# The expert loop's gelu is written back to PSUM, and the gating multiplies from there

## The chip, the core and the metric

The kernel runs on one core of a Trainium2 chip. The metric is the device time of one execution in microseconds (us). Three runs of the kernel before the change took 3090.99, 3093.1 and 3093.38 us; their median is 3093.1 us.

## The reference

One layer of a hybrid decoder for a prompt of 512 tokens (plus 16 learned ones) and 8 sampled tokens: RWKV-7 time mixing and differential attention side by side, gated, projected, and then a channel mixer with 16,384 experts of one neuron each. The change lies in that mixer alone:

```
q = (x @ peer_wq) ...; s = q . subkeys; top-16 of each half; top-16 of the 256 sums -> idx, gate
hid = einsum('td,thkd->thk', xb, u_tab[ib])
hid = gelu(hid, exact) * gate
out = einsum('thk,thkd->td', hid, v_tab[ib])
```

Each token uses 128 experts (8 heads of 16).

## The kernel before, in words

Everything is float32. TensorE products are made of float32r halves: a matrix is copied to a rounded "high" half, the difference is the "low" half, and three products (high by high, high by low, low by high) are summed in PSUM.

The expert mixer (`peer_experts`) treats 392 of the 520 token columns densely. For these, all 16,384 experts are computed, in 64 pairs of blocks of 128 experts. The gate matrix M of a pair, mostly zeros, comes from scratch memory. The remaining 128 tokens are treated row by row: in the first half of the loop (32 pairs) four rows of `peer_u` per pair are fetched by indirect DMA and multiplied with x (`few_dot`, L2038), and in the second half four rows of `peer_v` are fetched and added with their weights (`few_add`, L2054).

For one pair of the dense part, with e = 0, 1 the block in the pair, the steps are:

- TensorE transposes U in four steps into the PSUM tiles pU (`turn`, L1862). ScalarE copies each to the high half UH (`cut_u`, L1916), VectorE forms the low half UL (`rest_u`, L2023).
- TensorE computes the hidden values into the PSUM tile pH[e] (`product_u`, L1872, 24 matmuls for each e).
- ScalarE writes gelu of pH[e] to the SBUF tile G[e] (`gelu`, L1928). VectorE multiplies G[e] by M in place (`gate`, L2029). ScalarE copies G[e] to GH (`cut_g`, L1934), and GpSimd forms GL = G - GH (`rest_g`, L1971).
- ScalarE copies V to VH (`cut_v`, L1922), and GpSimd forms VL = V - VH, one instruction of 128x2048 (`rest_v`, L1975).
- TensorE multiplies VH, VL with GH, GL, eight output blocks of six matmuls each (`product_v`, L1883), and VectorE adds each block to the result (`add`, L2033).

The loop is pipelined over the pairs p, q = p+1 and r = p+2. Each engine has its own instruction queue, in an order written out by hand, and semaphores tie them together. In one step of the loop:

- TensorE: `product_u(q)`; then for n = 0 to 7 `product_v(p, n)`, with `turn(r, n/2)` ahead of each even n.
- ScalarE: `gelu(q,0)`, `cut_v(q)`, `cut_g(q,0)`, `gelu(q,1)`, `cut_u(r,0)`, `cut_g(q,1)`, `cut_u(r,1..3)`.
- VectorE: `gate(q,0)`, `gate(q,1)`; in the second half of the loop a small copy of 128x4 (`few_weigh`, L2047); then for even n `rest_u(r, n/2)` and `add(p,n)`, for odd n one `few_dot` or `few_add` and `add(p,n)`.
- GpSimd: `rest_v(q)`, `rest_g(q,0)`, `rest_g(q,1)`; then it waits until VectorE has used the four rows that share the buffer (the last `few_dot` or `few_add` of pair q), copies four row numbers (L1981), and issues four indirect DMAs (L1987) for pair q+2.
- SyncE issues the loads of U, M and V.

`product_v(p, n)` uses one of four PSUM tiles and so waits until `add(p, n-4)` is done; `turn(r, st)` with st of 2 or 3 waits for `rest_u(r, st-2)`.

Of the kernel before, what the change touches and what calls it, by code (L numbers as in the profile page):

```python
# [17 lines left out]
ALU = mybir.AluOpType  # L18
ACT = mybir.ActivationFunctionType
# [88 lines left out]
def sc(nc):  # L108
    return nc.scalar.activation
# [1325 lines left out]
ND = TQ - SPARSE  # L1435
# [323 lines left out]
def peer_experts(nc, ins, c, xh, xl, mscr, acc, few, spare):  # L1759
# [7 lines left out]
    with Stage(nc, "experts") as s:  # L1767
        U = [s.sb(f"U{b}", [P, 2, D]) for b in range(2)]
        V = [s.sb(f"V{b}", [P, 2, D]) for b in range(2)]
        M = [s.sb(f"M{b}", [P, 2, ND]) for b in range(2)]  # L1770
# [4 lines left out]
        G = [s.sb(f"G{e}", [P, ND]) for e in range(2)]  # L1775
# [9 lines left out]
        pH = [s.ps(f"pH{e}", [P, 512]) for e in range(2)]  # L1785
# [5 lines left out]
        turned, u_hi, u_lo, hidden, gelued, gated, g_hi, g_lo, v_hi, v_lo, summed, added = (  # L1791
            s.sem(n) for n in ("turned", "u_hi", "u_lo", "hidden", "gelued", "gated", "g_hi", "g_lo", "v_hi", "v_lo",
                               "summed", "added"))
# [71 lines left out]
        def product_u(pe, q):  # L1865
            for e in range(2):
                pe.wait_ge(u_lo, q.count(4, 2 * e + 2))
                if q.after(1):
                    pe.wait_ge(gelued, q.count(2, e - 1))
                for k in range(KD):  # L1870
                    for n, (u, x) in enumerate(((UH, xh), (UH, xl), (UL, xh))):
                        last = nc.tensor.matmul(pH[e][:, 0:ND], u[e][:, k, :], x[:, k, :], start=(k == 0 and n == 0),  # L1872
                                                stop=(k == KD - 1 and n == 2))
                last.then_inc(hidden, 1)
# [11 lines left out]
        @blk.tensor  # L1886
        def _(pe):
            def first():
                for st in range(4):
                    turn(pe, Pair(0), st)  # L1890
                product_u(pe, Pair(0))
                for st in range(4):
                    turn(pe, Pair(1), st)

            def body(p, q, r, rows_of_u):
                product_u(pe, q)
                for n in range(8):
                    if n % 2 == 0:
                        turn(pe, r, n // 2)
                    product_v(pe, p, n)  # L1900

            def tail():
                product_u(pe, Pair(NQ - 1))
                for p in (NQ - 2, NQ - 1):
                    for n in range(8):
                        product_v(pe, Pair(p), n)

            schedule(pe, first, body, tail)
# [14 lines left out]

        def gelu(act, q, e):
            act.wait_ge(hidden, q.count(2, e + 1))
            if q.after(1):
                act.wait_ge(g_lo, q.count(2, e - 1))
            sc(nc)(G[e][:, :], pH[e][:, 0:ND], ACT.Gelu).then_inc(gelued, 1)  # L1928

        def cut_g(act, q, e):  # L1930
            act.wait_ge(gated, q.count(2, e + 1))
# [5 lines left out]
        def _(act):  # L1937
            def hidden_values(q):
                gelu(act, q, 0)
                cut_v(act, q)  # L1940
                cut_g(act, q, 0)
                gelu(act, q, 1)
# [83 lines left out]
        def gate(dve, q, e):  # L2026
            dve.wait_ge(m_in[q.b], q.loads())
            dve.wait_ge(gelued, q.count(2, e + 1))
            nc.vector.tensor_tensor(G[e][:, :], G[e][:, :], M[q.b][:, e, :], ALU.mult).then_inc(gated, 1)  # L2029

        def add(dve, q, n):
            dve.wait_ge(summed, q.count(8, n + 1))
# [25 lines left out]
        def _(dve):  # L2058
            def first():
                dve.sem_inc(added, 4)  # L2060
                for st in range(4):
                    rest_u(dve, Pair(0), st)
                for e in range(2):
                    gate(dve, Pair(0), e)
                for st in range(4):
                    rest_u(dve, Pair(1), st)
                for n in range(NB):
                    few_dot(dve, Pair(0), n)
                few_keep(dve, Pair(0))

            def body(p, q, r, rows_of_u):
                for e in range(2):
                    gate(dve, q, e)
                if q.i is None and q.off == NQ // 2:
                    dve.wait_ge(few_gelued, 1)
                    nc.vector.tensor_tensor(hid[:, :], hid[:, :], few["gate"][:, :], ALU.mult).then_inc(few_gated, 1)
                    dve.wait_ge(few_gated, 1)
                if not rows_of_u:
                    few_weigh(dve, q)
                for n in range(8):  # L2080
                    if n % 2 == 0:
                        rest_u(dve, r, n // 2)
                    elif rows_of_u:
                        few_dot(dve, q, n // 2)
                    else:
                        few_add(dve, q, n // 2)
                    add(dve, p, n)
                if rows_of_u:
                    few_keep(dve, q)

            def tail():
                for e in range(2):
                    gate(dve, Pair(NQ - 1), e)
                few_weigh(dve, Pair(NQ - 1))
                for p in (NQ - 2, NQ - 1):
                    for n in range(8):
                        add(dve, Pair(p), n)
                        if p == NQ - 2 and n % 2:
                            few_add(dve, Pair(NQ - 1), n // 2)
# [178 lines left out]
```

## Time and profile before

| | us |
|---|---|
| median of 3 runs | 3093.1 |
| the profiled execution's own time | 3090.84 |
| its span in the trace | 3089.7 |
| PE busy | 2410.4 (78%) |
| DVE busy | 2033.2 (66%) |
| ACT busy | 775.1 (25%) |
| POOL busy | 1095.0 (35%) |

In the profile PE is TensorE (PEld its weight loads), DVE VectorE, ACT ScalarE, POOL GpSimd and SP SyncE. "Busy" is the time in which an engine executes an instruction, and an instruction's duration counts from its dispatch: time in which it is held up inside the engine counts as busy too. The expert loop takes the stretch from about 1640 us to 3076 us of the span, so it is nearly half of the kernel. The stretches before it are not touched by the change.

### The profile page before, as it was taken

To read this page: it belongs to the slowest core of one execution; us is meant where nothing else is said; L and a number is where in the kernel's file an instruction comes from. 1 tells how busy PE (TensorE), PEld (TensorE's weight loads), DVE (VectorE), ACT (ScalarE), POOL (GpSimd) and SP (SyncE) were. 2 spreads that over 40 slices of the span, in tenths; PEclk is the share of its full clock that TensorE was granted. 3 is DMA by queue.
4 is the path that set the end of the run, shared out by engine and by line. 5 is a ranking of instruction groups with operands and counts; after the bars stand their busy time and mean duration, and the time that the engine had idled before them with its cause. 6 is when DMAs were issued, how large, how long until landed. Compare 5 with 4: busy or idle time off the path is not lost. (4 is left out here: it accounts for less than half of the span.)

```text
span 3089.7 us, 49756 instructions
## 1 busy us (share of the span) xinstructions
PE 2410.4 (78%) x17079; PEld 2159.8 (70%) x17079; DVE 2033.2 (66%) x3749; ACT 775.1 (25%) x1389; POOL 1095.0 (35%) x1131
## 2 busy tenths in 40 slices
PE   4965885586969679604847999899988889889898
PEld 3964774244349678503637889888888888888887
DVE  3137554756731417998956776777778787787877
ACT  1111000122212211004953222222222222222221
POOL 2410000001313311326944545445454544545443
PEclk8976887665979889856978999999999999999999
DMA  2310000123812212100587556556555555555552
GB/s 65 88 36 1 3 3 21 41 83 101 271 46 72 70 55 62 34 0 0 138 194 285 205 201 214 204 201 211 199 199 211 206 198 200 201 207 205 199 199 94
DMA packets 207541, 403.48 MB, mean 131 GB/s; under 512 B 12798, under 2 KB 134073, under 8 KB 190810
## 3 DMA queue, kind: packets, MB, share of 16 engines
q1 hardware_dynamic: 165210, 251.21, 25.0%
q0 software_dynamic: 42240, 151.03, 14.6%
q8 instruction: 60, 0.98, 0.1%
q14 instruction: 31, 0.25, 0.0%
HBM read 370.81 MB, written 31.39 MB: 130 GB/s over the span
## 5 line engine op out<-in xcount | busy, mean ns | idle before, releaser
L2029 DVE TENSOR_TENSOR experts_G<-experts_G,experts_M 128x392 f32<-128x392 f32 x128 | 369.5, 2887 | 330.3 <-ACT experts_G L1928 330.2
L1883 PE MATMUL experts_pV<-experts_GH,experts_VH 128*128 128x392 f32 x1024 | 404.7, 395 | 27.9 <-DVE keep_xT L2033 27.2
L1883 PE MATMUL experts_pV<-experts_GL,experts_VH 128*128 128x392 f32 x1024 | 369.8, 361 | 0.0
L1883 PE MATMUL experts_pV<-experts_GH,experts_VL 128*128 128x392 f32 x1024 | 369.0, 360 | 0.0
L1872 PE MATMUL experts_pH<-keep_xh,experts_UH 128*128 128x392 f32 x1024 | 351.3, 343 | 0.0
L1872 PE MATMUL experts_pH<-keep_xl,experts_UH 128*128 128x392 f32 x1024 | 349.3, 341 | 0.0
L1872 PE MATMUL experts_pH<-keep_xh,experts_UL 128*128 128x392 f32 x1024 | 348.4, 340 | 0.0
L1975 POOL TENSOR_TENSOR experts_VL<-experts_V,experts_VH 128x2048 fp32r<-128x2048 f32 x64 | 295.3, 4614 | 19.3 <-ACT experts_VH L1922 18.0
L2033 DVE TENSOR_TENSOR keep_xT<-experts_pV,keep_xT 128x392 f32<-128x392 f32 x512 | 282.3, 552 | 1.6 <-PE experts_pV L1883 1.5
L1862 PE MATMUL experts_pU<-keep_ident,experts_U 128*128 128x128 f32 x1024 | 167.6, 290 | 117.2 <-DVE experts_UL L2023 109.0
L1883 PEld LDWEIGHTS experts_pV<-experts_GH,experts_VH 128*128 128x128 f32 x1024 | 208.2, 203 | 56.8 <-DVE keep_xT L2033 54.1
L1862 PEld LDWEIGHTS experts_pU<-keep_ident,experts_U 128*128 128x128 f32 x1024 | 132.2, 149 | 143.6 <-DVE experts_UL L2023 126.6
L1981 POOL COPY experts_at<-keep_few_row 128x4 uint32 (+1 forms) x64 | 11.8, 184 | 620.2 <-DVE experts_dot L2038 296.7
L1916 ACT ACTIVATE experts_UH<-experts_pU 128x512 fp32r<-128x512 f32 x256 | 151.7, 593 | 262.0 <-PE experts_pU L1862 262.0
L1883 PEld LDWEIGHTS experts_pV<-experts_GL,experts_VH 128*128 128x128 f32 x1024 | 210.6, 206 | 0.0
L1883 PEld LDWEIGHTS experts_pV<-experts_GH,experts_VL 128*128 128x128 f32 x1024 | 209.2, 204 | 0.0
L1872 PEld LDWEIGHTS experts_pH<-keep_xh,experts_UL 128*128 128x128 f32 x1024 | 192.9, 188 | 0.0
L1872 PEld LDWEIGHTS experts_pH<-keep_xh,experts_UH 128*128 128x128 f32 x1024 | 192.9, 188 | 0.0
L1872 PEld LDWEIGHTS experts_pH<-keep_xl,experts_UH 128*128 128x128 f32 x1024 | 192.8, 188 | 0.0
L1928 ACT ACTIVATE experts_G<-experts_pH 128x392 f32<-128x392 f32 x128 | 63.7, 497 | 481.7 <-PE experts_pH L1872 481.7
L2023 DVE TENSOR_TENSOR experts_UL<-experts_pU,experts_UH 128x512 fp32r<-128x512 f32 x256 | 173.1, 676 | 10.5 <-ACT experts_UH L1916 10.5
L1025 POOL IOTA att_dist<- 128x528 f32 x1 | 0.6, 572 | 460.2 <-POOLq L68 460.2
(424 smaller groups left out, 5164.3 us busy)
## 6 DMA issues: line engine op xcount, KB each, us to landing
experts_U<-in_peer_u SPq DMA_DIRECT2D x64, 1024.0 KB, 4.8
experts_V<-in_peer_v SPq DMA_DIRECT2D x64, 1024.0 KB, 5.2
experts_M<-scratch_gates SPq DMA_DIRECT2D x64, 392.0 KB, 3.2
keep_K<-in_cache_k SPq DMA_DIRECT2D x64, 256.0 KB, 3.1
keep_V<-in_cache_v POOLq DMA_DIRECT2D x64, 256.0 KB, 3.7
scratch_gates<-spread_M SPq DMA_DIRECT2D x2, 8192.0 KB, 33.0
inp_w<-in_w_in SPq DMA_DIRECT2D x22, 512.0 KB, 3.8
scratch_gates<-spread_M SPq DMA_DIRECT2D x1, 8704.0 KB, 35.6
```

What stands on the lines that cost most here:

```text
L1025: nc.gpsimd.iota(dist[:, :], pattern=[[-1, WM]], base=META + 3 * P, channel_multiplier=1, allow_small_or_imprecise_dtypes=True).then_inc(b ...
L1862: last = nc.tensor.transpose(pU[a][:, k, :], U[q.b][:, e, (4 * a + k) * P:(4 * a + k + 1) * P], c["ident"][:, :])
L1872: last = nc.tensor.matmul(pH[e][:, 0:ND], u[e][:, k, :], x[:, k, :], start=(k == 0 and n == 0), stop=(k == KD - 1 and n == 2))
L1883: last = nc.tensor.matmul(pV[n % 4][:, 0:ND], l, r, start=(t == 0), stop=(t == 5))
L1916: sc(nc)(UH[e][:, 4 * a:4 * a + 4, :], pU[a][:, :, :], ACT.Copy).then_inc(u_hi, 1)
L1928: sc(nc)(G[e][:, :], pH[e][:, 0:ND], ACT.Gelu).then_inc(gelued, 1)
L1975: nc.gpsimd.tensor_tensor(VL[q.b][:, :, :], V[q.b][:, :, :], VH[q.b][:, :, :].bitcast(F32), ALU.subtract).then_inc(v_lo, 1)
L1981: nc.gpsimd.tensor_copy(at[q.b][:, :], few["row"][:, bass.ds(q.count(NB, 0 if of_u else -SLOTS), NB)]).then_inc(staged, 1)
L2023: nc.vector.tensor_tensor(UL[e][:, 4 * a:4 * a + 4, :], pU[a][:, :, :], UH[e][:, 4 * a:4 * a + 4, :].bitcast(F32), ALU.subtract).then_inc( ...
L2029: nc.vector.tensor_tensor(G[e][:, :], G[e][:, :], M[q.b][:, e, :], ALU.mult).then_inc(gated, 1)
L2033: nc.vector.tensor_tensor(acc[:, n, :], pV[n % 4][:, 0:ND], acc[:, n, :], ALU.add).then_inc(added, 1)
```

## The change

The gelu no longer writes G[e] but overwrites its own input pH[e] in PSUM. The gating multiply reads pH[e] (PSUM) and M (SBUF) and writes G[e]. The waits follow the buffers: `product_u` of the next pair, which overwrites pH[e], waits for the gating (`gated`) where it waited for the gelu (`gelued`), and the wait for `rest_g` of the pair before (`g_lo`), which protects G[e], goes from the gelu on ScalarE to the gating on VectorE.

```diff
             for e in range(2):
                 pe.wait_ge(u_lo, q.count(4, 2 * e + 2))
                 if q.after(1):
-                    pe.wait_ge(gelued, q.count(2, e - 1))
+                    pe.wait_ge(gated, q.count(2, e - 1))
...
         def gelu(act, q, e):
             act.wait_ge(hidden, q.count(2, e + 1))
-            if q.after(1):
-                act.wait_ge(g_lo, q.count(2, e - 1))
-            sc(nc)(G[e][:, :], pH[e][:, 0:ND], ACT.Gelu).then_inc(gelued, 1)
+            sc(nc)(pH[e][:, 0:ND], pH[e][:, 0:ND], ACT.Gelu).then_inc(gelued, 1)
...
         def gate(dve, q, e):
             dve.wait_ge(m_in[q.b], q.loads())
             dve.wait_ge(gelued, q.count(2, e + 1))
-            nc.vector.tensor_tensor(G[e][:, :], G[e][:, :], M[q.b][:, e, :], ALU.mult).then_inc(gated, 1)
+            if q.after(1):
+                dve.wait_ge(g_lo, q.count(2, e - 1))
+            nc.vector.tensor_tensor(G[e][:, :], pH[e][:, 0:ND], M[q.b][:, e, :], ALU.mult).then_inc(gated, 1)
```

VectorE's queue at the head of a step of the loop, as a difference between before (-) and after (+). REGISTER_ALU and ISA rows are the queue's own preparation of waits:

```order
 L1825 UNCONDITIONAL_BRANCH
 L1825 ISA
-L2028 ISA
-L2029 TENSOR_TENSOR experts_G<-experts_G,experts_M 128x392
+L2026 ISA
 L2028 REGISTER_ALU
-L2029 TENSOR_TENSOR experts_G<-experts_G,experts_M 128x392
-L2022 ISA
-L2023 TENSOR_TENSOR experts_UL<-experts_pU,experts_UH 128x512
+L2029 TENSOR_TENSOR experts_G<-experts_pH,experts_M 128x392
+L2026 REGISTER_ALU
```

The compute instructions stand in the same order on every engine; only the gating's first operand and the place of one wait are new.

## Rows read from the trace of the kernel before

**Rows 1.** The page's costliest groups: busy us, mean ns of one, idle before
```profile
L2029 DVE TENSOR_TENSOR experts_G<-experts_G,experts_M 128x392 f32<-128x392 f32 x128 | 369.5, 2887 | 330.3 <-ACT experts_G L1928 330.2
...
L2033 DVE TENSOR_TENSOR keep_xT<-experts_pV,keep_xT 128x392 f32<-128x392 f32 x512 | 282.3, 552 | 1.6 <-PE experts_pV L1883 1.5
```
**Rows 2.** Timeline, all engines, pair at 1994 us: start, duration, instruction, idle before
```profile
1991.89 0.52 ACT L1934 ACTIVATE experts_GH<-experts_G 128x392 fp32r<-128x392 f32 x1
...
1994.53 6.07 DVE L2029 TENSOR_TENSOR experts_G<-experts_G,experts_M 128x392 f32<-128x392 f32 x1 [3.73 <-ACT experts_G L1928]
1994.59 4.61 POOL L1975 TENSOR_TENSOR experts_VL<-experts_V,experts_VH 128x2048 fp32r<-128x2048 f32 x1
...
1999.15 1.01 POOL L1971 TENSOR_TENSOR experts_GL<-experts_G,experts_GH 128x392 fp32r<-128x392 f32 x1
...
2001.24 1.04 POOL L1971 TENSOR_TENSOR experts_GL<-experts_G,experts_GH 128x392 fp32r<-128x392 f32 x1 [1.07 <-ACT experts_GH L1934]
...
2001.59 1.76 DVE L2038 CUSTOM_DVE_ANT_0 keep_xn<-keep_xn,keep_few_x 128x1024 f32<-128x1024 f32 x1
...
2010.21 1.21 DVE L2038 CUSTOM_DVE_ANT_0 keep_xn<-keep_xn,keep_few_x 128x1024 f32<-128x1024 f32 x1
...
2011.61 0.18 POOL L1981 COPY experts_at<-keep_few_row 128x4 uint32 x1 [9.33 <-DVE experts_dot L2038]
...
2017.12 4.63 POOL L1975 TENSOR_TENSOR experts_VL<-experts_V,experts_VH 128x2048 fp32r<-128x2048 f32 x1
```
**Rows 3.** Stretches of each half, L1975 alone: from:to, length, busy (count), clock
```profile
1683.40:2354.50 671.10, 138.42 (x30) 0.94 0.59 205
2354.50:3035.80 681.30, 138.54 (x30) 0.95 0.58 201
```
**Rows 4.** Timeline, TensorE: the first transposes of three successive steps, and one inner wait
```profile
2197.81 0.60 PE L1862 MATMUL experts_pU<-keep_ident,experts_U 128*128 128x128 f32 x4
...
2217.20 0.60 PE L1862 MATMUL experts_pU<-keep_ident,experts_U 128*128 128x128 f32 x4
...
2224.65 0.66 PE L1862 MATMUL experts_pU<-keep_ident,experts_U 128*128 128x128 f32 x4 [2.14 <-DVE experts_UL L2023]
...
2242.19 0.60 PE L1862 MATMUL experts_pU<-keep_ident,experts_U 128*128 128x128 f32 x4
```
**Rows 5.** Timeline, the loop's second pair, where a row product stands behind the port
```profile
1661.21 0.53 ACT L1934 ACTIVATE experts_GH<-experts_G 128x392 fp32r<-128x392 f32 x1
...
1662.06 4.60 POOL L1975 TENSOR_TENSOR experts_VL<-experts_V,experts_VH 128x2048 fp32r<-128x2048 f32 x1
1662.18 7.50 DVE L2038 CUSTOM_DVE_ANT_0 experts_R<-experts_R,keep_few_x 128x1024 f32<-128x1024 f32 x1
...
1666.61 1.97 POOL L1971 TENSOR_TENSOR experts_GL<-experts_G,experts_GH 128x392 fp32r<-128x392 f32 x2
```
**Rows 6.** Timeline, a pair in which the gating comes late
```profile
2196.00 0.52 ACT L1934 ACTIVATE experts_GH<-experts_G 128x392 fp32r<-128x392 f32 x1
2196.18 4.61 POOL L1975 TENSOR_TENSOR experts_VL<-experts_V,experts_VH 128x2048 fp32r<-128x2048 f32 x1
...
2198.62 2.60 DVE L2029 TENSOR_TENSOR experts_G<-experts_G,experts_M 128x392 f32<-128x392 f32 x1 [3.72 <-ACT experts_G L1928]
```
**Rows 7.** Timeline, the last pair: the small copy of 128x4
```profile
3060.58 2.35 POOL L1971 TENSOR_TENSOR experts_GL<-experts_G,experts_GH 128x392 fp32r<-128x392 f32 x2
3060.98 1.00 DVE L2047 COPY experts_dot<-experts_hid 128x4 f32<-128x4 f32 x1
```
**Rows 8.** Timeline, a pair of the second half
```profile
2604.01 4.63 POOL L1975 TENSOR_TENSOR experts_VL<-experts_V,experts_VH 128x2048 fp32r<-128x2048 f32 x1
...
2609.96 0.16 DVE L2047 COPY experts_dot<-experts_hid 128x4 f32 x1
...
2611.10 1.68 DVE L2054 SCALAR_TENSOR_TENSOR keep_few_y<-experts_R,experts_dot,keep_few_y 128x1024 f32<-128x1024 f32 x1
...
2626.82 4.62 POOL L1975 TENSOR_TENSOR experts_VL<-experts_V,experts_VH 128x2048 fp32r<-128x2048 f32 x1
```

## The prediction

> **What bounds the kernel now.** I read the costliest groups first, then the timeline of single steps of the expert loop on all engines, and last TensorE's own rows.
>
> The costliest VectorE group is the gating, L2029: 128 instructions with a mean of 2887 ns, beside L2033, which has the same shape, one operand in PSUM, and a mean of 552 ns over 512 instructions [rows 1]. A mean so far from that of a like instruction asks for the single ones. The step at 1994 us shows one: the gating of the second block is dispatched at 1994.53 and ends at 2000.60, 6.07 us later [rows 2]. GpSimd's split of V runs from 1994.59 to 1999.20, its first `rest_g` from 1999.15 to 2000.16, and the gating ends 0.44 us after that. So it does not compute for 6 us; it is held until GpSimd stops, and then takes its own half microsecond. Both read two operands from SBUF. The row product (`few_dot`) shows the same: dispatched at 2001.59 under GpSimd's second `rest_g` (to 2002.28), it takes 1.76 us against 1.21 us when GpSimd is quiet [rows 2]. L2033, which reads PSUM and one SBUF operand, shows nothing of the kind in its mean [rows 1].
>
> What sets the period of the loop is a ring through both engines. GpSimd starts the split of V at v = 1994.59. VectorE is held, and finishes its first row product at 2003.35, which is v + 8.76. Three further rounds bring the last row product to 2011.42, 8.07 us later (2.69 us a round). GpSimd, idle for 9.33 us until then, copies row numbers at 2011.61, issues four indirect DMAs, and starts the next split at 2017.12 [rows 2]: 5.70 us after the last row product. 8.76 + 8.07 + 5.70 = 22.53 us, the distance from v to v. The stretches give means of 671.10/30 = 22.37 us for the first half and 681.30/30 = 22.71 us for the second [rows 3]. The first is a bit below 22.53 because some steps have a late gating, as in [rows 6].
>
> TensorE is not the one that sets it: from 2197.81 to 2217.20 a step took 19.39 us, and the next 24.99 us, with a wait of 2.14 us for `rest_u` in it [rows 4]. The long step also ran in part at a lower clock: the granted clock of the stretches is 0.94 and 0.95 of the full 2.4 GHz [rows 3].
>
> **The change, part by part.**
>
> *The gelu* writes PSUM instead of SBUF. No row before shows ScalarE writing PSUM. The reads and writes of like size all lie near half a microsecond (the 128x392 copy at 1991.89 took 0.52 us [rows 2]), and I take no difference, with 0.2 us either way as bounds. It isn't in the ring: what follows it on VectorE is held by GpSimd for about 4 us more, so a later or earlier gelu moves nothing. Cost 0.
>
> *The waits.* TensorE's wait for the gating of the pair before is satisfied well before: TensorE writes pH again only behind the eight output blocks and four transposes of the step, and the gating is done by the middle of these (2201.22 against 2197.81, with the step's 19.39 us [rows 4, 6]). VectorE's new wait for `rest_g` of the pair before is for an instruction that ended at v + 7.69 (2002.28 [rows 2]), while the next step's gatings stand behind the eight adds and four row products, which end at 2011.42 or later. Behind the gating in VectorE's queue stand `rest_u`, the adds and the row products, so it would be dear if late, but it has that slack. Cost 0.
>
> *The gating itself* has now one SBUF operand, as L2033 has, so I price it at 0.55 us [rows 1] and free of the hold. For the block e = 0 nothing changes. For e = 1, 5.5 us leave VectorE's busy time in a fully held step.
>
> *What is late next.* The gating was only the first instruction to meet GpSimd's splits. The next instruction on VectorE with two SBUF operands now stands there.
>
> First half of the loop: after the gating come `rest_u` and `add`, 0.99 us from the gating's end to the row product's dispatch (2000.60 to 2001.59 [rows 2]), and neither is held. The row product is then dispatched about 0.55 + 0.99 = 1.5 us after the gating is, while the split of V still runs. That this instruction is held too is seen at 1662.18: 7.50 us, until both `rest_g` are through at 1668.58, and 1.10 us more [rows 5]. How many of GpSimd's three instructions it must let pass decides the gain. In [rows 2] the gating let two pass (both ready before v; the copy GH for the first was done at 1992.41). In [rows 5] all three were ready before v (GH of the second block was done at 1661.74), and all three passed. In [rows 6] the first `rest_g` became ready at 2196.52, 0.34 us after v, and the gating passed ahead of it, ending at 2201.22, 0.43 after the split. So I read: those of GpSimd's instructions go ahead that were ready when the split began. After the change GH of the second block is ready about 0.55 + 0.5 us after the gating's dispatch, and the gating comes 0.8 us after TensorE's first transpose of the step (2198.62 against 2197.81 [rows 4, 6]), that is near v as now. So the second `rest_g` is ready about 1 us after v, and two instructions pass. The row product ends at 5.57 (2000.16 - 1994.59) + 1.10 = v + 6.67. That is 8.76 - 6.67 = 2.09 us less than now, so the period is 20.44 us. Against the mean: (22.37 - 20.44) x 30 = 58 us.
>
> Second half: here the small copy L2047 stands between gating and `rest_u`. It reads one SBUF operand, but it is held as well: in the last pair it took 1.00 us under a `rest_g` [rows 7], against 0.16 us in [rows 8]. Now it comes after the long hold; after the change it comes first and takes the hold over. It ends near v + 5.6, and `few_add` is dispatched 1.14 us behind it (2609.96 to 2611.10 [rows 8]), at v + 6.71. The second `rest_g` runs meanwhile and is through by then. `few_add` takes 1.27 us when not held (the 1.68 in the row is held by the `rest_g` there; 1.21 is the like product of [rows 2], and I take 1.27 as 1.21 plus 5%, an estimate), so it ends at v + 7.98 against v + 8.77 now (2611.10 + 1.68 - 2604.01). The gain is 0.79 x 30 = 24 us.
>
> The Trainium skill, page "SBUF — State Buffer", section "Who interferes with whom", says that GpSimd shares a port pair with VectorE, that a VectorE instruction with two SBUF inputs, or a copy in a two-port mode, is blocked whole by a GpSimd one that reads SBUF, and that one with a single SBUF input outside these modes is not. The rows agree, the 1.00 us copy included. It also says that whoever issues first gets the pair. By that rule the second `rest_g`, ready before the row product is dispatched, would pass too; that is the first rival below.
>
> *The sum.* 58 + 24 = 82 us off the profiled execution's own 3090.84 us gives 3009 us. The median of the three runs is 2.3 us above that execution, so 3011 us. TensorE's 19.39 us lies below both new periods (20.4 and 21.9 us), so it does not cap the gain; at the loop's two ends TensorE is the bound or the steps are few, and I count nothing.
>
> **The rivals.**
>
> *All three of GpSimd's instructions pass.* For: [rows 5] has it. Against: they were all ready there before v, which [rows 6] suggests matters. The first row product would end at v + 7.62 (1669.68 - 1662.06): the period is 22.53 - 1.14 = 21.39, a gain of 0.98 x 30 = 29 us. In the second half the copy would end at v + 6.5 and `few_add` at 6.52 + 1.14 + 1.27 = v + 8.93, 0.16 us later than now, a loss of 5 us. Together 24 us: 3069 us.
>
> *More gets free.* In [rows 6] the gating, dispatched 2.44 us after v, passed after the split alone. If the row product does too, it ends at 4.6 + 1.1 = v + 5.7, then meets the second `rest_g` with its next product at about v + 7.7, and that one ends near v + 8.8 in place of 9.4; the period is 19.9 us, the gain of the first half 74 us, the second at 24 to 56 us: 2963 to 2995, say 2978 us. Were the copy not held at all, the second half would gain 2.0 x 30 = 60 us beside 58: 2975 us, the same neighbourhood.
>
> *TensorE becomes the bound* at 19.39 us a step, because GpSimd's four DMAs or the row products come early enough: (22.54 - 19.39) x 60 = 189 us, 2904 us. Against: the ring has 13.77 us beside the held piece, and nothing of it is touched.
>
> *The gating stays held* although it reads PSUM: then nothing changes, 3093 us. L2033's mean speaks against it.
>
> *Slower: TensorE's clock.* Waits inside each step may cost the clock. The step of 24.99 us had more than 2.14 us of waiting and then ran partly at half clock; against 19.39 it lost 24.99 - 19.39 - 2.14 = 3.46 us beyond that wait. Now such a step is followed by a short one, and the mean stays at 22.5. If the new hold, which falls once in every step on the row product and so on the adds that TensorE waits for, brought every step to 24.99 us, the loop would lose (24.99 - 22.54) x 60 = 147 us: 3240 us. It decides from the point at which TensorE's own step, with waits and low clock, is longer than the ring. Against: TensorE's wait shrinks by as much as its work stretches, since GpSimd's start depends on VectorE's and not on TensorE's pace.
>
> **How the numbers follow.** The forecast has 0.50, all three pass 0.21, more free 0.16, TensorE the bound 0.03, nothing changes 0.04, slower 0.04; 0.02 is left for cases unnamed. The forecast's own spread is about 15 us either way (1 us of error in one half's period is 30 us). The range 2965 to 3070 us takes in the forecast, the first rival's value, and most of the third case's. A change under 0.2%, or 6 us, could not be told from none. Faster 0.92, same 0.03, slower 0.05.
>
> **What would show it.** The gating's mean falls from 2887 to about 555 ns. The first row product of each step in the first half grows to about 5 us. In the second half the copy L2047 grows from 0.16 to about 5 us. GpSimd's idle before L1981 falls by the gain, and the splits of V follow each other at 20.4 and 21.9 us. If L2047 stays at 0.16, the second half is mispriced; if the row product ends at v + 7.6, the first rival holds; if TensorE's clock falls below 0.94 with longer steps, the last one.

## The result: 3059.0 us, two fifths of the gain that was forecast

The changed kernel takes 3059.0 us (median of 4 runs, 3058.19 to 3060.7), the kernel before, run beside it, 3092.05 us. The ratio is 0.9895, with a 95% interval of 0.9878 to 0.9912. It is faster by 33 us, where 82 us were forecast. The time lies in the range, near its slow end.

The groups that answer to [rows 1], from the page of the changed kernel; the third is the small copy of the loop's second half:

```profile
L2029 DVE TENSOR_TENSOR experts_G<-experts_pH,experts_M 128x392 f32<-128x392 f32 x128 | 72.5, 567 | 326.4 <-ACT experts_pH L1926 322.2
L2033 DVE TENSOR_TENSOR keep_xT<-experts_pV,keep_xT 128x392 f32<-128x392 f32 x512 | 282.6, 553 | 1.6 <-PE experts_pV L1883 1.5
...
L2047 DVE COPY experts_dot<-experts_hid 128x4 f32 (+1 forms) x32 | 171.0, 5344 | 0.0
```

The gating fell from a mean of 2887 ns to 567 ns, as forecast: 297 us of busy time are gone from that line. VectorE's busy time as a whole only fell from 2033.2 to 2006.6 us. The hold moved on. In the second half the copy of 128x4 carries it, 5344 ns a piece.

The timeline of a step in the first half, all engines (answers to [rows 2]):

```profile
2000.93 4.63 POOL L1973 TENSOR_TENSOR experts_VL<-experts_V,experts_VH 128x2048 fp32r<-128x2048 f32 x1
2000.94 0.57 DVE L2029 TENSOR_TENSOR experts_G<-experts_pH,experts_M 128x392 f32<-128x392 f32 x1 [3.73 <-ACT experts_pH L1926]
...
2001.54 0.53 ACT L1932 ACTIVATE experts_GH<-experts_G 128x392 fp32r<-128x392 f32 x1 [0.17 <-DVE experts_G L2029]
...
2002.49 6.11 DVE L2038 CUSTOM_DVE_ANT_0 experts_R<-experts_R,keep_few_x 128x1024 f32<-128x1024 f32 x1
...
2005.51 2.00 POOL L1969 TENSOR_TENSOR experts_GL<-experts_G,experts_GH 128x392 fp32r<-128x392 f32 x2
...
2015.46 1.21 DVE L2038 CUSTOM_DVE_ANT_0 experts_R<-experts_R,keep_few_x 128x1024 f32<-128x1024 f32 x1
2016.85 0.18 POOL L1979 COPY experts_at<-keep_few_row 128x4 uint32 x1 [9.34 <-DVE experts_dot L2038]
...
2022.37 4.64 POOL L1973 TENSOR_TENSOR experts_VL<-experts_V,experts_VH 128x2048 fp32r<-128x2048 f32 x1
```

With v = 2000.93 for the start of the split of V (GpSimd's L1973), the gating beside it is no longer held: 0.57 us. `rest_u` and `add` aren't either. The row product, dispatched at v + 1.56, is held until both `rest_g` are through (2007.51) and ends at 2008.60, v + 7.67. The forecast had v + 6.67, with only the first `rest_g` ahead of it. The rest of the ring is as it was: three rounds to 2016.67 (8.07 us) and 5.70 us to the next split at 2022.37, a period of 21.44 us.

The second half, a step of it (answers to [rows 8]):

```profile
2619.41 4.60 POOL L1973 TENSOR_TENSOR experts_VL<-experts_V,experts_VH 128x2048 fp32r<-128x2048 f32 x1
...
2620.94 5.05 DVE L2047 COPY experts_dot<-experts_hid 128x4 f32 x1
2621.05 0.53 ACT L1932 ACTIVATE experts_GH<-experts_G 128x392 fp32r<-128x392 f32 x1 [0.17 <-DVE experts_G L2029]
...
2623.97 1.99 POOL L1969 TENSOR_TENSOR experts_GL<-experts_G,experts_GH 128x392 fp32r<-128x392 f32 x2
...
2626.98 1.27 DVE L2054 SCALAR_TENSOR_TENSOR keep_few_y<-experts_R,experts_dot,keep_few_y 128x1024 f32<-128x1024 f32 x1
```

The copy ends at v + 6.58, behind both `rest_g`, although the second of these got its data (GH, done at 2621.58) only after the copy was dispatched (2620.94), and `few_add` at v + 8.84. It was v + 8.77 before. So the second half gained nothing. The stretches of 30 periods each say so (columns as in [rows 3]; these answer to its two rows):

```profile
1681.00:2323.40 642.40, 138.57 (x30) 0.98 0.62 215
2323.40:3006.00 682.60, 138.40 (x30) 0.95 0.58 200
```

The first half fell from 671.10 to 642.40 us (21.41 us a step), and the second went from 681.30 to 682.60 us (22.75 us). That is 27.4 us. The spans differ by 30.1 us, and the other 2.7 us lie at the loop's ends, 2.4 of them ahead of the first stretch.

### The profile page after: what moved, and what is told of

It reads as the page before. It is cut to its first block and busy times, and to the rows that moved or that the text cites. A ratio compares the mean times of both kernels' runs of the same rounds, so it can differ in the third digit from the quotient of the medians.

```text
span 3059.6 us, 49750 instructions
## 1 busy us (share of the span) xinstructions
PE 2386.2 (78%) x17079; PEld 2144.9 (70%) x17079; DVE 2006.6 (66%) x3749; ACT 783.6 (26%) x1389; POOL 1086.9 (36%) x1131
## 5 line engine op out<-in xcount | busy, mean ns | idle before, releaser
L1883 PE MATMUL experts_pV<-experts_GH,experts_VH 128*128 128x392 f32 x1024 | 397.2, 388 | 60.5 <-DVE keep_xT L2033 60.3
L1883 PE MATMUL experts_pV<-experts_GL,experts_VH 128*128 128x392 f32 x1024 | 362.9, 354 | 0.0
L1973 POOL TENSOR_TENSOR experts_VL<-experts_V,experts_VH 128x2048 fp32r<-128x2048 f32 x64 | 295.3, 4614 | 20.6 <-ACT experts_VH L1922 19.3
L2029 DVE TENSOR_TENSOR experts_G<-experts_pH,experts_M 128x392 f32<-128x392 f32 x128 | 72.5, 567 | 326.4 <-ACT experts_pH L1926 322.2
L1926 ACT ACTIVATE experts_pH<-experts_pH 128x392 f32<-128x392 f32 x128 | 61.7, 482 | 477.9 <-PE experts_pH L1872 477.9
L2047 DVE COPY experts_dot<-experts_hid 128x4 f32 (+1 forms) x32 | 171.0, 5344 | 0.0
```

The source lines that it names most:

```text
L1883: last = nc.tensor.matmul(pV[n % 4][:, 0:ND], l, r, start=(t == 0), stop=(t == 5))
L1926: sc(nc)(pH[e][:, 0:ND], pH[e][:, 0:ND], ACT.Gelu).then_inc(gelued, 1)
L1973: nc.gpsimd.tensor_tensor(VL[q.b][:, :, :], V[q.b][:, :, :], VH[q.b][:, :, :].bitcast(F32), ALU.subtract).then_inc(v_lo, 1)
L2029: nc.vector.tensor_tensor(G[e][:, :], pH[e][:, 0:ND], M[q.b][:, e, :], ALU.mult).then_inc(gated, 1)
L2047: nc.vector.tensor_copy(dot[q.b][:, :], hid[:, bass.ds(q.count(NB, -SLOTS), NB)]).then_inc(weighed, 1)
```

## The experiments

Theory A, formed from the result: GpSimd runs on from one instruction to the next, without letting a held VectorE instruction in, if the next was ready when the one ahead of it started. If it became ready later, VectorE gets in between. Theory B, its rival: whatever GpSimd has left goes first, ready or not. A third reading is first come, first served, the ground of the prediction's first rival; the rows above and below decide on it. The second question is whether the ring (split of V, held VectorE instruction, row products, row fetch, next split) sets the period. All ratios are against the kernel before, run on the same chip.

### The second rest_g made ready late (cutg_late)

```diff
-                cut_u(act, r, 0)
+                for st in range(3):
+                    cut_u(act, r, st)
                 cut_g(act, q, 1)
-                for st in range(1, 4):
-                    cut_u(act, r, st)
+                cut_u(act, r, 3)
```

> The changed kernel, but ScalarE makes GH of the second block only behind its third cut_u, so that the second rest_g is not ready before the first has ended. This sets up the premise of the forecast. If the period is the ring through GpSimd and the row products, the first row product ends at v + 6.7, the periods are 20.4 us in the first half and 21.9 us in the second, 3003 us. If something else (TensorE's waits and its clock, the adds) sets the period, moving this copy changes it by less than 10 us in all.

Measured: 3005.15 us, ratio 0.9715 (0.9699 to 0.9732). Its timeline in the first half, and its stretches:

```profile
2090.98 4.63 POOL L1973 TENSOR_TENSOR experts_VL<-experts_V,experts_VH 128x2048 fp32r<-128x2048 f32 x1
...
2092.56 5.12 DVE L2038 CUSTOM_DVE_ANT_0 keep_xn<-keep_xn,keep_few_x 128x1024 f32<-128x1024 f32 x1
...
2095.57 1.02 POOL L1969 TENSOR_TENSOR experts_GL<-experts_G,experts_GH 128x392 fp32r<-128x392 f32 x1
...
2096.50 0.52 ACT L1932 ACTIVATE experts_GH<-experts_G 128x392 fp32r<-128x392 f32 x1
2097.10 1.48 POOL L1969 TENSOR_TENSOR experts_GL<-experts_G,experts_GH 128x392 fp32r<-128x392 f32 x1 [0.51 <-ACT experts_GH L1932]
```

```profile
1681.60:2297.50 615.90, 138.60 (x30) 1.00 0.66 224
2297.50:2951.30 653.80, 138.42 (x30) 0.97 0.61 209
```

The expectation of 3003 us is met. GH is done at 2097.02, when the first `rest_g` is already over (2096.59), and the row product ends at 2097.68, v + 6.70. The periods are 20.5 and 21.8 us. These are the forecast's own figures (6.67; 20.44 and 21.92), and the time is within 6 us of its 3011. The ring's arithmetic holds. What was wrong is only which of GpSimd's instructions goes ahead.

One later step of the same run comes out differently, and tells theory A from both the forecast's reading and first come, first served:

```profile
2194.90 7.83 DVE L2038 CUSTOM_DVE_ANT_0 experts_R<-experts_R,keep_few_x 128x1024 f32<-128x1024 f32 x1
2195.10 4.62 POOL L1973 TENSOR_TENSOR experts_VL<-experts_V,experts_VH 128x2048 fp32r<-128x2048 f32 x1
...
2198.84 0.52 ACT L1932 ACTIVATE experts_GH<-experts_G 128x392 fp32r<-128x392 f32 x1
2199.63 2.01 POOL L1969 TENSOR_TENSOR experts_GL<-experts_G,experts_GH 128x392 fp32r<-128x392 f32 x2
```

GH of the second block is done at 2199.36. That is 4.26 us after v, long after the row product was dispatched (2194.90), and 0.27 us before the first `rest_g` starts. All three of GpSimd's instructions pass, and the row product ends at v + 7.63.

### Each rest_g waits for the GpSimd instruction ahead (self_wait)

```diff
             pool.wait_ge(g_hi, q.count(2, e + 1))
+            if e == 0:
+                pool.wait_ge(v_lo, q.count(1, 1))
+            else:
+                pool.wait_ge(g_lo, q.count(2, 1))
```

> The changed kernel, but GpSimd's two rest_g each wait for the completion of the GpSimd instruction ahead of them, so they are never ready when it starts. Theory A (a GpSimd instruction that is ready when its predecessor starts is run on without letting the held VectorE instruction in; one that becomes ready later lets it in): the held instruction gets in behind the split of V, at v + 4.6. First half: first row product ends at v + 5.7, period about 19.9 us. Second half: the copy ends at v + 4.7, few_add is dispatched at v + 5.8, period 20.9 us if it gets in ahead of the second rest_g, 22.0 us if not. In all 2957 to 2990 us. Theory B (whatever GpSimd has left goes first, ready or not at the start): still held until v + 6.6, periods as in the changed kernel or 0.1 us longer, 3059 to 3065 us.

Measured: 2957.66 us, ratio 0.9564 (0.9548 to 0.958). Its timeline in the first half:

```profile
2058.40 4.65 POOL L1977 TENSOR_TENSOR experts_VL<-experts_V,experts_VH 128x2048 fp32r<-128x2048 f32 x1
...
2059.97 4.16 DVE L2042 CUSTOM_DVE_ANT_0 experts_R<-experts_R,keep_few_x 128x1024 f32<-128x1024 f32 x1
...
2063.19 3.01 POOL L1973 TENSOR_TENSOR experts_GL<-experts_G,experts_GH 128x392 fp32r<-128x392 f32 x2
...
2065.62 1.66 DVE L2042 CUSTOM_DVE_ANT_0 experts_R<-experts_R,keep_few_x 128x1024 f32<-128x1024 f32 x1
```

The row product is dispatched 1.57 us after v, as in the changed kernel, and ends at 2064.13, v + 5.73, in place of v + 7.67. Nothing but GpSimd's waits on itself is different. Theory B falls. First come, first served would give this result too, since `rest_g` may now start only at v + 4.6. The next product then meets a `rest_g` and takes 1.66 us. The 30 periods of each half take 599.30 and 625.70 us, 19.98 and 20.86 us a step; 19.9 and 20.9 (or 22.0) were expected.

### The same waits on the kernel before (before_self_wait)

The edit is the same as for self_wait, on the kernel whose gating stays in SBUF.

> The kernel before (gelu and gating in SBUF), with GpSimd's two rest_g waiting for the completion of the GpSimd instruction ahead, as was tried on the changed kernel. Theory A (readiness at the predecessor's start decides): the gating is let in behind the split of V and ends at v + 5.03 in every step, where it was v + 6.01. The periods fall to 21.0 to 22.0 us in the first half and about 22.3 us in the second, 3040 to 3070 us. Theory B (what GpSimd has left goes first): 3093 us.

Measured: 3033.35 us, ratio 0.981 (0.9794 to 0.9826). The gating is dispatched at 2102.85 and let in behind the split:

```profile
2102.85 5.10 DVE L2033 TENSOR_TENSOR experts_G<-experts_G,experts_M 128x392 f32<-128x392 f32 x1 [3.71 <-ACT experts_G L1928]
2102.89 4.62 POOL L1979 TENSOR_TENSOR experts_VL<-experts_V,experts_VH 128x2048 fp32r<-128x2048 f32 x1
```

It ends at v + 5.06, where it was v + 6.01 in [rows 2]. The periods are 21.0 us (630.60/30) and 22.2 us (666.40/30), at the low ends of what was expected. The total came out 7 us below the expected range: the two halves are 40.5 and 14.9 us shorter, 55 us together, and the range had been drawn too high for them. Theory A holds on this kernel too. These two waits alone are worth more than the change under study (3033 against 3059 us).

### The small copy moved to ScalarE (weigh_act)

```diff
+        def few_weigh(act, q):
+            act.wait_ge(few_gated, 1)
+            act.wait_ge(used, q.count(NB, -NB))
+            sc(nc)(dot[q.b][:, :], hid[:, bass.ds(q.count(NB, -SLOTS), NB)], ACT.Copy).then_inc(weighed, 1)
...
                 cut_u(act, r, 0)
+                if not rows_of_u:
+                    few_weigh(act, q)
                 cut_g(act, q, 1)
...
-                if not rows_of_u:
-                    few_weigh(dve, q)
```

> The changed kernel, but the small copy of 128x4 (few_weigh) is made by ScalarE, behind its cut_u of the step. If that copy on VectorE is what brings the hold ahead of rest_u in the second half, few_add now meets the hold itself, as the row product does in the first half: it ends at v + 7.7 in place of v + 8.84, the second half's period goes from 22.76 to about 21.7 us, 3027 us in all, the first half unchanged. If few_add is late there for another reason, 3059 us.

Measured: 3027.86 us, ratio 0.9796 (0.978 to 0.9812). A step of the second half:

```profile
2604.83 4.62 POOL L1981 TENSOR_TENSOR experts_VL<-experts_V,experts_VH 128x2048 fp32r<-128x2048 f32 x1
2605.07 0.20 ACT L1937 ACTIVATE experts_dot<-experts_hid 128x4 f32 x1
...
2606.30 6.20 DVE L2058 SCALAR_TENSOR_TENSOR keep_few_y<-experts_R,experts_dot,keep_few_y 128x1024 f32<-128x1024 f32 x1
```

ScalarE's copy takes 0.20 us beside the split, not held. `few_add` now carries the hold and ends at v + 7.67 (was 8.84). The second half's 30 periods take 648.10 us, 21.6 a step (was 22.75), the first half's 642.60. So the copy on VectorE was what ate the second half's gain. 3027 us were expected.

### The change for the second block alone (e1_only)

The edit is shown against the changed kernel.

```diff
-                    pe.wait_ge(gated, q.count(2, e - 1))
+                    pe.wait_ge(gated if e else gelued, q.count(2, e - 1))
...
+            if e == 0 and q.after(1):
+                act.wait_ge(g_lo, q.count(2, e - 1))
-            sc(nc)(pH[e][:, 0:ND], pH[e][:, 0:ND], ACT.Gelu).then_inc(gelued, 1)
+            sc(nc)(pH[e][:, 0:ND] if e else G[e][:, :], pH[e][:, 0:ND], ACT.Gelu).then_inc(gelued, 1)
...
-            if q.after(1):
+            if e and q.after(1):
                 dve.wait_ge(g_lo, q.count(2, e - 1))
-            nc.vector.tensor_tensor(G[e][:, :], pH[e][:, 0:ND], M[q.b][:, e, :], ALU.mult).then_inc(gated, 1)
+            nc.vector.tensor_tensor(G[e][:, :], pH[e][:, 0:ND] if e else G[e][:, :], M[q.b][:, e, :], ALU.mult).then_inc(gated, 1)
```

> The change made for the second block of each pair alone (e = 1); the first block's gelu and gating stay in SBUF with their old waits. The first block's gating never met GpSimd, so by the port account this is worth all that the whole change is: 3059 us, within 3 us. If half of the gain comes from each block (a cheaper PSUM operand, the moved waits), 3075 us.

Measured: 3062.94 us, ratio 0.9905 (0.9888 to 0.9921), which overlaps the changed kernel's interval. It lies 4 us above the changed kernel where at most 3 were expected. The four runs of each don't overlap (3061.86 to 3066.52 against 3058.19 to 3060.7), but they were not taken side by side, so whether the first block's part is worth these 4 us or nothing stays open. Some 30 of the 33 us belong to the second block, and 3075 us is excluded.

### The row fetch one step later in GpSimd's queue (rows_later, before_rows_later)

```diff
             def first():
...
                 halves_of(Pair(0))
-                rows_of(Pair(2), True)
             def body(p, q, r, rows_of_u):
                 halves_of(q)
                 if q.i is not None:
-                    rows_of(Pair(q.off + 2, q.i), rows_of_u)
-                elif q.off + 2 < NQ:
-                    rows_of(Pair(q.off + 2), q.off + 2 < NQ // 2)
+                    rows_of(Pair(q.off + 1, q.i), rows_of_u)
+                elif q.off + 1 < NQ:
+                    rows_of(Pair(q.off + 1), q.off + 1 < NQ // 2)
```

The fetch for a pair now stands behind the splits of the pair just ahead of it, when VectorE has long used the buffer. On the changed kernel:

> The changed kernel, but GpSimd issues the fetch of a pair's rows one step later in its queue, behind the splits of the next pair, where VectorE's use of the buffer is long past. Ring theory: GpSimd waits for nothing of VectorE any more, the split of V starts as soon as VH is there, about 1.7 us ahead of TensorE's first transpose of the step, and TensorE's own 19.4 us become the period: 2897 us. Rival (the held VectorE instructions themselves are what costs, not GpSimd's wait): period stays at 21.4 and 22.8 us, 3059 us.

Measured: 2864.01 us, ratio 0.9263 (0.9247 to 0.9278), 33 us less than the 2897 us of the ring theory. On the kernel before:

> The kernel before, with the same move of the row fetch. Ring theory: also near TensorE's 19.4 us a step, about 2904 us, since the gating is then asked for 2.4 us after v and let in behind the split of V, at v + 5.0, which TensorE does not notice; the change to the gelu would be worth less than 10 us here. Rival: the gating's hold costs by itself, so this stays at 3092 us, or at least 30 us above the same move on the changed kernel.

Measured: 2902.07 us, ratio 0.9385 (0.937 to 0.9401). The timeline of rows_later, first half:

```profile
2068.50 4.61 POOL L1973 TENSOR_TENSOR experts_VL<-experts_V,experts_VH 128x2048 fp32r<-128x2048 f32 x1 [4.02 <-ACT experts_VH L1922]
...
2071.02 0.57 DVE L2028 TENSOR_TENSOR experts_G<-experts_pH,experts_M 128x392 f32<-128x392 f32 x1 [3.73 <-ACT experts_pH L1926]
...
2072.57 1.62 DVE L2037 CUSTOM_DVE_ANT_0 experts_R<-experts_R,keep_few_x 128x1024 f32<-128x1024 f32 x1
```

GpSimd waits 4.02 us for ScalarE's VH and for nothing of VectorE. The row product, dispatched at v + 4.07, takes 1.62 us in place of 6.11: it gets in behind the split, ahead of the first `rest_g`. The stretches of both kernels, rows_later first:

```profile
1671.90:2238.40 566.50, 138.62 (x30) 1.00 0.67 243
2238.40:2808.70 570.30, 138.48 (x30) 1.00 0.70 240
```

```profile
1678.30:2257.90 579.60, 138.01 (x30) 1.00 0.65 238
2257.90:2846.40 588.50, 138.18 (x30) 1.00 0.63 233
```

They are 18.88 and 19.01 us a step on the changed kernel, 19.32 and 19.62 us on the kernel before, with the clock granted in full (2.4 GHz) in both. The ring was the bound: without it TensorE is. In a stretch of rows_later it is busy all the time (the view's columns: length, TensorE busy, count, clock):

```profile
1700.00:2300.00 600.00, 600.00 (x3556) 1.00 0.67 243
```

In before_rows_later the gating is still held a little:

```profile
2084.15 4.61 POOL L1975 TENSOR_TENSOR experts_VL<-experts_V,experts_VH 128x2048 fp32r<-128x2048 f32 x1 [5.16 <-ACT experts_VH L1922]
...
2086.60 2.58 DVE L2028 TENSOR_TENSOR experts_G<-experts_G,experts_M 128x392 f32<-128x392 f32 x1 [3.73 <-ACT experts_G L1928]
```

The expectation that the gelu's change would be worth less than 10 us here was wrong: it is worth 38 us (2902.07 - 2864.01), which is what the rival had (at least 30 us). TensorE's 19.39 us in [rows 4], which I had taken as its own pace, was no such thing. In that step the fourth group of transposes starts 2.94 us after the third, and in the step above it starts 2.91 us after, where it is 2.57 us in rows_later. That the delay comes from the adds behind a late gating is argued from this, not tested. TensorE's own pace is 18.88 us, and that is also why rows_later came out 33 us under its expectation.

### Both: row fetch later, copy on ScalarE (rows_weigh)

The edits are those of rows_later and weigh_act together.

> The changed kernel with the row fetch issued one step later (as in rows_later) and the small copy on ScalarE. TensorE sets the period already at 18.9 us in the first half and 19.0 us in the second. The copy is held there until v + 4.64 and costs TensorE some 0.1 us a step: 2860 us, against 2864 us without this. If the copy costs nothing there, 2864 us.

Measured: 2861.58 us, ratio 0.9254 (0.9239 to 0.927). By the starts of the splits, 30 steps of the second half take 566.65 us (2242.71 to 2809.36), 18.89 us each, against 19.01 us, so the copy's 0.1 us a step is seen there. In the whole time (2860 us expected) 2.4 us can't be told from none. Both this and rows_later beat the changed kernel by about 195 us.

## Why the prediction was wrong, point by point

**What bounds the loop: right.** The ring (from v to the end of the first row product, then three rounds, then 5.70 us) gave the period in every kernel that kept it. The first piece was 8.76, 7.67, 6.70 us at periods of 22.53, 21.44, 20.48 us in steps of the first half (before, changed, cutg_late). Taking the ring apart gave 2864 us. TensorE's own step was overstated (19.39 against 18.88 us), which the sum did not use.

**The gating itself, the gelu and the waits: right.** The gating's mean is 567 ns (550 expected). The gelu took 497 ns before and 482 ns now. In e1_only the first block's share is 4 us at most.

**What is late next: right in place, wrong in size.** The row product and the copy took over the hold, as said. The step that failed is the sentence "those of GpSimd's instructions go ahead that were ready when the split began". I read it from three cases [rows 2, 5, 6] which another rule fits as well: ready when the instruction just ahead starts. In the changed kernel the second `rest_g` becomes ready at 2002.07, 1.14 us after v, so by my rule it stood behind the row product; but the first `rest_g` starts only at 2005.51, so it was ready by then and passed. The row product ends at v + 7.67 and not v + 6.67. That is 1.0 us of the 2.09 us in the first half: 30 x (21.41 - 20.44) = 29 us of the 58. In the second half `few_add` ends at v + 8.84 and not at 7.98: 30 x (22.75 - 21.92) = 25 us, all of that term. Together 54 us, and 2.7 us came back at the loop's ends: 82 - 54 + 3 = 31 us, against 30.1 us in the spans. The cost of the gating, the ring and the order of VectorE's queue were right; these two terms, 58 and 24 us, measured 29 and -1 us.

cutg_late restores the forecast's premise and gives the forecast's time; self_wait and before_self_wait show the rule from the other side. That the next instruction's readiness near the start of the one ahead decides is shown; the prediction's reading had the wrong start.

**The first rival is what happened.** All three passed. Its period of 21.39 us was met (21.41). For the second half it had 22.87 us, and 22.75 was measured. Its 3069 us came out at 3059: 3.6 us from that half's smaller loss, 2.7 us from the loop's ends, and the rest is the spread of the medians. It stood on the rule of the Trainium skill, page "SBUF — State Buffer", section "Who interferes with whom", that whoever issues first gets the port pair. For the time of this kernel it gave the better answer than my reading. The traces don't bear the rule out as a matter of who asks first, in either direction. In [rows 6], and in the step of rows_later, a VectorE instruction dispatched after the first `rest_g` had its data went ahead of it. And in 31 of the 61 steps of the changed kernel in which all three pass, the held VectorE instruction was dispatched before GH of the second block was done, as in the step at 2619.41, and both `rest_g` still went first. So the rival's number was near for a reason that is only in part its own.

**The range.** I gave 0.50 to a reading that three rows suggested and drew the range at 3070 to 2965. 3059 lies inside it because it was drawn to the first rival's time; the forecast itself was not met, with 33 of 82 us of its gain.

**TensorE's clock** did not cost: the granted clock rose from 0.94 to 0.98 of 2.4 GHz in the first half, and stayed at 0.95 in the second, and the first rival's period held without any term for it.

## What to carry to other kernels

When VectorE and GpSimd run side by side, look for an instruction whose duration is far from its like in the same profile (2887 against 552 ns). Here that was a hold, and freeing the one instruction handed the hold to the next with two SBUF operands, or to a small SBUF copy. Price the change at that next instruction. Before that, look for the ring that turns the hold into time: here it ran through GpSimd's row fetch, and moving that fetch one step later is worth 195 us beside the 33 us of the change. Where a run of ready GpSimd instructions holds VectorE, let each wait for the completion of the one ahead: that alone took the changed kernel from 3059 to 2958 us and the kernel before from 3093 to 3033 us.

## What the runs showed of the hardware that I had not expected

GpSimd's instructions pass a held VectorE instruction as a train: in the changed kernel one of 4.6 us and two of 1.0 us, although VectorE had asked 4 us before the last began (2002.49 against about 2006.5). The train is cut where a GpSimd instruction was not ready by about the start of its predecessor: with waits on completion the held instruction got in at v + 4.6 every time (self_wait, before_self_wait). The cut is not exactly at that start. GH of the first block done 0.20 us after v still let its `rest_g` pass, in weigh_act:

```profile
1680.60 0.52 ACT L1932 ACTIVATE experts_GH<-experts_G 128x392 fp32r<-128x392 f32 x1
1680.92 4.63 POOL L1981 TENSOR_TENSOR experts_VL<-experts_V,experts_VH 128x2048 fp32r<-128x2048 f32 x1
...
1684.85 3.76 DVE L2046 CUSTOM_DVE_ANT_0 keep_xn<-keep_xn,keep_few_x 128x1024 f32<-128x1024 f32 x1
```

(the row product ends at v + 7.69), and done 0.26 us after v it did not, in the kernel before:

```profile
1728.31 0.52 ACT L1934 ACTIVATE experts_GH<-experts_G 128x392 fp32r<-128x392 f32 x1
1728.57 4.60 POOL L1975 TENSOR_TENSOR experts_VL<-experts_V,experts_VH 128x2048 fp32r<-128x2048 f32 x1
...
1730.94 2.66 DVE L2029 TENSOR_TENSOR experts_G<-experts_G,experts_M 128x392 f32<-128x392 f32 x1 [3.73 <-ACT experts_G L1928]
```

(the gating ends at v + 5.03). With the cut between these two, theory A gives the number of GpSimd instructions that pass, as read from the held instruction's end, in all 504 steps with a held VectorE instruction, over the eight traces of kernels without the added waits. What on the chip makes this so (a look ahead of one instruction, or a hold on the port that is only given up when nothing is queued) no run here tells apart.

A VectorE copy of four elements a partition, with one SBUF source, is held just as an operation on two sources is: 5.05 us in place of 0.16. The same copy on ScalarE took 0.20 us beside the same split.
